# Two places of a weight ring exchanged, and the state part's preparation placed between the input blocks of a second mixer

## The chip, the cores and the metric

One core of a Trainium2 chip runs the whole program. The metric is the time of one execution on the device in microseconds (us), as the median of three runs.

## What is computed

The reference is two transformer-like blocks in a row, for 256 tokens of width 1024, in float32. Cut to what matters here:

```
x = first_block(x, ...)      # mixer (attention + rwkv7), then f = (silu(h@w_ffn_gate) * (h@w_ffn_up)) @ w_ffn_down
mod = silu(c) @ w_ada + b_ada               # six vectors of 1024: shifts, scales, gates
h = rms_norm(x) * (1 + sc1) + sh1
u, z, xbc, dt_raw = split(h @ w_in, ...)    # 256, 768, 1792 and 12 columns
y_pool = (pooled mean of u - u) @ w_pool * pool_scale
xbc = silu(causal_conv4(xbc) + bias)        # x: 768 channels, B: 512, C: 512
dt = softplus(dt_raw + dt_bias);  a_cs = cumsum(dt * -exp(a_log)) in chunks of 128 tokens
decay[l, s] = exp(a_cs[l] - a_cs[s]), l >= s          # per head, 12 heads
y = ((C B^T) * decay) @ (x * dt)  +  C @ state * exp(a_cs)   + x * d_skip
y = rms_norm_per_group(y * silu(z)) * norm_w
x = x + g1 * (concat(y_pool, y) @ w_out)
x = x + g2 * hier_moe(modulate(x))          # 32 experts, top 2 of one group of 8
out = rms_norm(x) * final_norm_w
```

## The kernel before

Everything runs from one hand-written program per engine; semaphores order them. There are 8 banks of matmul output memory. `plan_banks` lists all uses of the banks in the order in which TensorE writes them; use n is bank n mod 8, and TensorE may write it only when the use 8 places earlier has been read out.

**The ring of weights.** The list `W` names all weight blocks (up to 2 MB each) in the order of use, and SyncE (SP) loads block n into place `n % RING` of three. Before it issues a load, it waits until the last use of the block that lay in that place. SP works in order: a load that waits holds up all loads behind it. Around the feed-forward part the list is ... `("wo", 1)`, `("ff", 0)`, `("ada", 4)`, `("ff", 1)`, `("ff", 2)`, `("ff", 3)`, ... A block `("ff", c)` holds 256 gate and 256 up columns; `("ada", 4)` is a block of the modulation weights, used by TensorE in `ada_chunk(4)` just before the feed-forward part, while `("ff", 0)` is used by its first two of 22 steps.

**High and low parts.** Most products are made in three passes from rounded parts of both operands (lines 792 to 794). For each such block ScalarE (ACT) writes the rounded high part (`high_parts`, line 1684, two halves), and VectorE (DVE) writes the low part in place of the block in the ring (`low_part`, line 569, two halves). TensorE waits for the low part in `halved`.

**The second mixer.** Its input weights are six blocks `("in2", c)`, c = 0 to 5; 0 and 1 give `u` and `z`, two further blocks of 256 channels (`("xb", j)`, j = 0 to 6) lie in each of c = 2, 3, 4, and c = 5 (1072 KB) holds `("xb", 6)` and the 12 dt columns. TensorE makes `xb` 0 to 6; for each, ACT copies the bank into `xraw` and writes a scaled copy into `xs` (lines 1942 and 1945), DVE adds the three other taps of the convolution in six instructions (line 2583), and ACT applies silu (line 1952, the last at 1954). Then the dt product `("dt2",)` is made token by token with 12 columns a matmul, followed by the pooling `("pl",)` (lines 1336, 1338), `ada_chunk(6)` (line 969), the cumulative sums `("cs",)` (lines 1345, 1346), the pooled map `("pm",)` (1351), the decay rows `("rb", i, q)` (line 1359; DVE reads them at 2609, ACT takes the exponential at 1973), the products C B^T `("cb", i)` (line 1367; DVE masks them at 2616 and multiplies the decay by them at 2620), transposes of x and B (line 1373; ACT copies at 1978, DVE scales by dt at 2624), and the first product of the scan, `y_diag(0)` (line 1388). The latter needs the decay times C B^T and the scaled x. Two halves of the token rows (i = 0, 1) follow, then the output product `("mx", i, n)`, the norm and the router.

**The experts.** After the mixer SP streams the weights of 32 experts through two sets of buffers, one in the ring and one in the arena. The first set is loaded after the mixer's last norm sums and after `mx`; each later load waits for TensorE's use of the one before (`next_w13`, line 674; `next_w2`, line 680).

## Time and profile before

| what | value |
|---|---|
| median of 3 runs | 1127.08 us (1125.91 to 1128.21) |
| the profiled execution | 1125.6 us |
| its span, first to last instruction | 1123.8 us |
| TensorE (PE) busy | 1048.3 us, 93% of the span |
| DVE, ACT, GpSimd (POOL) busy | 462.5, 353.3, 39.6 us |
| HBM read | 314.37 MB |
| mean granted TensorE clock | 0.99 of full |
| chain that ended last | PE 70%, DMA 21%, DVE 4%, ACT 2% |

The table is from the profile's page. Times in the rows further down count from the first instruction of the span. "Busy" is the time in which an engine had an instruction at work; the idle time in square brackets behind a row is how long the engine stood before it, and "<-" names what released it. A clock of 1.00 is TensorE's upper level, 2.4 GHz, and 0.50 its lower one, 1.2 GHz.

### The profile page before, as it was taken

The page shows a single profiled execution, that of the slowest core. Times are in us where ns is not written, and L with a number is a line of the kernel's source. Part 1 is how long each engine was busy: PE and PEld are TensorE (multiplying, and loading weights), DVE is VectorE, ACT ScalarE, POOL GpSimd, SP SyncE. Part 2 cuts the span into 40 slices and gives each one's busy share as a digit, 9 for nine tenths or more (in the row PEclk, how much of TensorE's full clock was granted, in tenths as well). Part 3 has the DMA queues.
Part 4 walks back from the last instruction along what each step waited for, and adds up shares of the span by engine and source line. Part 5 has one row for each costly group of instructions (what it writes and reads, how often), then busy time and mean ns, then how long its engine had stood idle before and what let it go on. Part 6 is the DMA issues. An engine that isn't in the chain of part 4 may idle for free.

```text
span 1123.8 us, 17871 instructions
## 1 busy us (share of the span) xinstructions
PE 1048.3 (93%) x7527; PEld 717.3 (64%) x7527; DVE 462.5 (41%) x699; ACT 353.3 (31%) x507; POOL 39.6 (4%) x32
## 2 busy tenths in 40 slices
PE   6999999999989999999999999999899989898986
PEld 5996779899789998867986453443244333242432
DVE  4784245567634544356757351222122212121212
ACT  5752323554444444265542220111011111010102
POOL 0002200002000100000000000000000000000000
PEclk9999999999989999999989999999999999999999
DMA  9454371147474636675366869999999999999994
GB/s 324 157 203 159 110 247 60 71 155 265 148 225 152 216 122 228 232 288 181 119 222 244 363 255 422 420 423 421 422 423 421 422 422 423 421 422 422 422 421 191
DMA packets 95301, 316.36 MB, mean 282 GB/s; under 512 B 8118, under 2 KB 33030, under 8 KB 70534
## 3 DMA queue, kind: packets, MB, share of 16 engines
q1 hardware_dynamic: 94198, 312.75, 72.2%
q10 hardware_dynamic: 1040, 2.69, 0.7%
q8 instruction: 50, 0.82, 0.3%
q14 instruction: 13, 0.11, 0.0%
HBM read 314.37 MB, written 1.05 MB: 281 GB/s over the span
## 4 chain that ended last, share of the span: by engine, by line
PE 70%; DMA 21%; DVE 4%; ACT 2%; issue 1%; SPq 0%; POOL 0%; DVEq 0%; ACTq 0%
DMA arena<-in_w 20%; PE bank L1513 12%; PE bank L792 11%; PE bank L794 11%; PE bank L793 11%; PE bank L1537 4%; PE bank L778 4%; PE bank L1053 3%; PE bank L969 1%; PE bank L1493 1%; PE bank L1002 1%; PE bank L769 1%; PE bank L1550 1%; PE bank L739 1%; DVE ring_low L569 1%
## 5 line engine op out<-in xcount | busy, mean ns | idle before, releaser
L1513 PE MATMUL bank<-ring,hT 128*64 128x512 f32 x512 | 226.6, 594 | 28.7 <-DMA arena<-in_w 27.6
L1513 PE MATMUL bank<-arena,hT 128*64 128x512 f32 x512 | 226.7, 594 | 0.0
L794 PE MATMUL bank<-h_high,ring_low 128*128 128x256 f32 x688 | 194.1, 282 | 0.0
L1513 PEld LDWEIGHTS bank<-ring,hT 128*64 128x64 f32 x512 | 67.9, 137 | 180.4 <-issue 130.6
L569 DVE TENSOR_TENSOR ring_low<-ring,hi_high 128x2048 fp32r<-128x2048 f32 (+2 forms) x58 | 126.3, 2220 | 106.2 <-ACT hi_high L1684 106.2
L792 PE MATMUL bank<-h_high,hi_high 128*128 128x256 f32 x528 | 150.1, 284 | 4.9 <-DVE ring_low L569 4.2
L793 PE MATMUL bank<-h_low,hi_high 128*128 128x256 f32 x528 | 148.7, 282 | 0.0
L1684 ACT ACTIVATE hi_high<-ring 128x2048 fp32r<-128x2048 f32 (+2 forms) x58 | 104.6, 1853 | 101.8 <-DMA ring<-in_w_ffn_up 45.1
L794 PEld LDWEIGHTS bank<-h_high,ring_low 128*128 128x128 f32 x688 | 131.2, 191 | 0.0
L1537 PE MATMUL bank<-arena 128*64 128x512 f32 x384 | 113.3, 595 | 7.1 <-DVE hT L2821 6.7
L2827 DVE TENSOR_TENSOR arena<-arena,bank 128x512 f32<-128x512 f32 x16 | 17.3, 1083 | 229.3 <-ACT arena L2045 229.3
L792 PEld LDWEIGHTS bank<-h_high,hi_high 128*128 128x128 f32 x528 | 100.5, 190 | 6.3 <-DVE ring_low L569 4.4
L793 PEld LDWEIGHTS bank<-h_low,hi_high 128*128 128x128 f32 x528 | 100.8, 191 | 0.3 <-issue 0.2
L2045 ACT ACTIVATE arena<-bank 128x512 f32<-128x512 f32 x16 | 9.6, 599 | 231.1 <-PE bank L1513 231.1
L1513 PEld LDWEIGHTS bank<-arena,hT 128*64 128x64 f32 x512 | 67.9, 137 | 0.0
L1537 PEld LDWEIGHTS bank<-arena 128*64 128x64 f32 x384 | 35.1, 137 | 40.5 <-issue 39.5
L1537 PE MATMUL bank<-ring,arena 128*64 128x512 f32 x128 | 56.6, 595 | 4.3 <-ACT arena L2049 4.3
L2841 DVE SCALAR_TENSOR_TENSOR con<-bank,small,arena 128x512 f32<-128x512 f32 x32 | 24.0, 751 | 86.3 <-PE bank L1537 86.3
L2054 ACT ACTIVATE y_high<-con 128x512 fp32r<-128x512 f32 x32 | 20.2, 631 | 125.1 <-DVE con L2841 125.1
L792 PE MATMUL bank<-h_high,hrw_high 128*128 128x256 f32 x160 | 45.8, 286 | 0.5 <-DVE ring_low L569 0.5
L793 PE MATMUL bank<-h_low,hrw_high 128*128 128x256 f32 x160 | 45.3, 283 | 0.0
L1537 PEld LDWEIGHTS bank<-ring,arena 128*64 128x64 f32 x128 | 16.9, 137 | 37.6 <-issue 36.1
(404 smaller groups left out, 1694.2 us busy)
## 6 DMA issues: line engine op xcount, KB each, us to landing
arena<-in_w SPq DMA_DIRECT2D x112, 1024.0 KB, 22.7
ring<-in_w SPq DMA_DIRECT2D x80, 1024.0 KB, 20.3
ring<-in_w_in SPq DMA_DIRECT2D x12, 2048.0 KB, 8.3
ring<-in_w_ada SPq DMA_DIRECT2D x8, 2048.0 KB, 8.2
ring<-in_w_ffn_gate SPq DMA_DIRECT2D x11, 1024.0 KB, 5.5
ring<-in_w_ffn_up SPq DMA_DIRECT2D x11, 1024.0 KB, 8.7
ring<-in_w_ffn_down SPq DMA_DIRECT2D x5, 2048.0 KB, 7.9
ring<-in_w_in SPq DMA_DIRECT2D x12, 512.0 KB, 4.6
```

Source lines behind the costliest of these rows:

```text
L569: return eng.tensor_tensor(ring_lo[:, r, c0:c1], ring[:, r, c0:c1], high_of(n)[:, c0:c1].bitcast(F32), ALU.subtract)
L778: last = mm(ps[:, 0:512], lhs[k][:, i * P:(i + 1) * P], w[:, k, 0:512], start=(k == 0), stop=(k == nk - 1))
L792: mm(ps, a[0], b[0], start=start, stop=False)
L793: mm(ps, a[0], b[1], start=False, stop=False)
L794: return mm(ps, a[1], b[0], start=False, stop=stop)
L1053: last = mm(ps[r, j * w:(j + 1) * w], left(4 * q + j, r), right(4 * q + j, r), start=True, stop=True)
L1513: last = mm(both(6 + half, x), hg[:, k, (2 * q + x) * CAP:(2 * q + x + 1) * CAP], w13s[x][k // 4][:, k % 4, half * EF:(half + 1) * EF], st ...
L1537: last = mm(both(4 + n, x), acT[:, 0, f, x * CAP:(x + 1) * CAP], w2s[q][x][f // 2][:, f % 2, n * 512:(n + 1) * 512], start=(f == 0), stop= ...
L1684: A_(high_of(n)[:, f], ring[:, r, f], ACT.Copy).then_inc(S("high"), 1)
L2054: A_(y_hi[n], y_out[:, n, :], ACT.Copy).then_inc(S("y_high"), 1)
L2827: V.tensor_tensor(by_row(ac[:, 0, :]), in_rows(sa[:, 0, :]), in_rows(bank[7][:, :]), ALU.mult).then_inc(S("ac"), 1)
L2841: V.scalar_tensor_tensor(y_out[:, n, :], bank[4 + n][:, :], slot_gate[:, 0:1], g2[:, n * 512:(n + 1) * 512], ALU.mult, ALU.mult).then_inc( ...
```

## The change

1. From `("ff", 2)` on, ring places 1 and 2 are exchanged (`ring_slot`). `("ff", 2)` now lies where `("ada", 4)` was, and `("ff", 3)` where `("ff", 0)` was. All later blocks keep their distance of three.
2. The input blocks of the second mixer are loaded in the order 0, 1, 5, 4, 3, 2, and `xb` is made from 6 down to 0, so that C, B and the dt columns come first.
3. The dt product is made channel by channel (24 matmuls of 256 columns over the last 128 columns of the block, then a copy by ACT and two transposes) instead of 48 matmuls of 12 columns.
4. dt, the pooling, the cumulative sums, the decay rows and C B^T stand between the `xb` blocks on all three engines.
5. The low parts of the last two blocks, in2 3 and in2 2, are split: DVE makes the first half, GpSimd the second.
6. Buffers move in the arena (`dec`, `cbm`, `dif`, `acs`, `ysq` and others), since they now live at the same time as the weights' high parts; `ada_chunk(6)` comes behind `xb` 0, and `ada_sum(6)` before the last transposes.

```diff
+IN2 = (0, 1, 5, 4, 3, 2)
...
-        for c in range(6):
+        for c in IN2:
             stream(("in2", c), [(0, cols(w_in2, c * 512, min(c * 512 + 512, w_in2.shape[1])))],
-                   ("uz", 1, c) if c < 2 else ("xb", 2 * c - 3) if c < 5 else ("dt2",))
+                   ("uz", 1, c) if c < 2 else ("xb", 2 * c - 4))
...
+        keys = [key for key, _, _ in W]
+        turned, kept = (keys.index(key) % RING for key in (("ada", 4), ("ff", 0)))
+
+        def ring_slot(n):
+
+            return {turned: kept, kept: turned}.get(n % RING, n % RING) if n >= keys.index(("ff", 2)) else n % RING
...
             for n, (key, parts, last) in enumerate(W):
-                r = n % RING
+                r = ring_slot(n)
...
-                    pe.wait_ge(S("in2_low"), 2 * (n - BY_TWO) + 2)
+                    pos = n - BY_TWO
+                    pe.wait_ge(S("in2_low"), 2 * pos + 2 if pos < 4 else pos + 5)
+                    if pos >= 4:
+                        pe.wait_ge(S("in2_pool"), pos - 3)
```

TensorE's program from the end of `uz`, with the new functions' bodies as before except `dt_rows` (the removed lines are those that stood behind `xb`):

```diff
+            def dt_rows():
+
+                halved(("in2", 5))
+                w = parts_view(("in2", 5), "p (k c) -> p k c", k=KD)
+                ps = write(pe, ("dt2",))
+                for k in range(KD):
+                    last = by_parts(ps[:, 0:SEQ], [x[:, k, DT_AT:DT_AT + P] for x in w], (hT_hi[2][:, k, :], hT_lo[:, k, :]),
+                                    k == 0, k == KD - 1)
+                last.then_inc(*full(("dt2",)))
...
+            dt_rows()
+            xb(6)
+            drained(pe, ("dt2",))
+            transposes(("dtt",), [(i, dtrow[:, i * P:(i + 1) * P]) for i in range(NT)])
+            xb(5)
+            pooled()
+            xb(4)
+            decay_sums()
+            decay_rows(0)
+            xb(3)
+            decay_rows(1)
+            xb(2)
+            xb(1)
+            pe.wait_ge(S("xs"), 4)
             for i in range(NT):
...
+                gram(i)
+            xb(0)
+            ada_chunk(6)
+            pe.wait_ge(S("xs"), 5)
             for i in range(NT):
...
+                x_tokens(i, 1)
```

ACT's, DVE's and GpSimd's programs, cut to the order of the calls (`raw` is the copy and the scaled copy of a bank, `silu_of` the silu of the n-th block made, `conv` the six taps):

```diff
+            ps = filled(act, ("dt2",))
+            A_(dtrow, ps[:, 0:SEQ], ACT.Copy).then_inc(*free(("dt2",)))
+            high_parts(BY_TWO + 4)
+            raw(6)
...
+            raw(5)
+            high_parts(BY_TWO + 5)
+            silu_of(0)
+            raw(4)
+            silu_of(1)
+            raw(3)
+            silu_of(2)
...
+            decay_exp(0)
+            raw(2)
+            decay_exp(1)
+            silu_of(3)
+            raw(1)
+            silu_of(4)
+            silu_of(5)
+            raw(0)
+            ada_rows(6)
+            for i in range(NT):
+                tokens_out(i, 1)
+            silu_of(6)
...
+            for n in (BY_TWO + 4, BY_TWO + 5):
+                _, words = split_words(n)
+                pool.wait_ge(S("high"), 2 * n + 2)
+                low_part(nc.gpsimd, n, words // 2, words).then_inc(S("in2_pool"), 1)
...
+            first_half_low(BY_TWO + 4)
+            conv(6)
...
+            conv(5)
+            first_half_low(BY_TWO + 5)
...
+            decays(0)
+            conv(4)
+            conv(3)
+            decays(1)
+            conv(2)
+            conv(1)
```

The order on two engines, as the built programs have it (instructions in program order; the same line has a number some 13 to 45 higher on TensorE and some 10 to 95 higher on DVE in the changed kernel; `con` holds constants, `arena` the buffers, `bank` the matmul outputs).

TensorE, before, from `ada_chunk(6)` behind the pooling up to `y_diag(0)`:

```order
L969 MATMUL bank<-ring,arena 32x512 x8
L1345 MATMUL bank<-arena,con 128x12 x2
L1346 MATMUL bank<-arena,con 128x12
L1351 MATMUL bank<-arena 64x256 x4
L1359 MATMUL bank<-con,arena 128x128 x24
L1367 MATMUL bank<-arena 128x128 x8
L1373 MATMUL bank<-con,arena 128x128 x16
L939 MATMUL bank<-con,arena 64x1 x8
L969 MATMUL bank<-ring,arena 32x512 x8
L1388 MATMUL bank<-arena 128x64 x12
```

TensorE, changed, from the end of the last block `xb` 0 (L805 to L807) up to `y_diag(0)` (L1433):

```order
L806 MATMUL bank<-h_low,hi_high_49 128x256
L807 MATMUL bank<-h_high,ring_low 128x256
L982 MATMUL bank<-ring,arena 32x512 x8
L1351 MATMUL bank<-con,arena 128x128 x4
L1417 MATMUL bank<-arena 64x256 x4
L1351 MATMUL bank<-con,arena 128x128 x4
L952 MATMUL bank<-con,arena 64x1 x8
L1351 MATMUL bank<-con,arena 128x128 x8
L982 MATMUL bank<-ring,arena 32x512 x8
L1433 MATMUL bank<-arena 128x64 x12
```

The sums, decay rows and C B^T (L1345, L1359, L1367 before) no longer stand between the last block and `y_diag(0)`; the transposes, the modulation chunks and the pooled map do.

DVE, before, from the last block's convolution on:

```order
L2583 SCALAR_TENSOR_TENSOR arena<-arena,parcol 128x255 x2
L2583 SCALAR_TENSOR_TENSOR arena<-arena,parcol 128x254 x2
L2583 SCALAR_TENSOR_TENSOR arena<-arena,parcol 128x253 x2
L2591 TENSOR_TENSOR arena<-bank,small 128x2x12
L2594 SCALAR_TENSOR_TENSOR arena<-arena 128x2x12
L2596 COPY arena<-bank 128x512
L2598 SCALAR_TENSOR_TENSOR arena<-arena 128x2x12
L2600 SCALAR_TENSOR_TENSOR arena<-arena,small 128x2x12
L2602 COPY arena<-bank 128x3x12
L2609 TENSOR_SCALAR arena<-bank,arena 128x128 x24
L2616 TENSOR_TENSOR arena<-bank,con 128x512
L2620 TENSOR_TENSOR arena<-arena 128x1536
```

DVE, changed, from the dt step on (L2684 is the old L2591, L2664 the convolution's old L2583, L579 the low part's old L569):

```order
L2684 TENSOR_TENSOR arena<-bank,small 128x2x12
L2687 SCALAR_TENSOR_TENSOR arena<-arena 128x2x12
L579 TENSOR_TENSOR ring_low<-ring,hi_high_51 128x2048
L2664 SCALAR_TENSOR_TENSOR arena<-arena,parcol 128x255 x2
L2664 SCALAR_TENSOR_TENSOR arena<-arena,parcol 128x254 x2
L2664 SCALAR_TENSOR_TENSOR arena<-arena,parcol 128x253 x2
L2691 SCALAR_TENSOR_TENSOR arena<-arena 128x2x12
L2693 SCALAR_TENSOR_TENSOR arena<-arena,small 128x2x12
L2664 SCALAR_TENSOR_TENSOR arena<-arena,parcol 128x255 x2
L2664 SCALAR_TENSOR_TENSOR arena<-arena,parcol 128x254 x2
L2664 SCALAR_TENSOR_TENSOR arena<-arena,parcol 128x253 x2
L579 TENSOR_TENSOR ring_low<-ring,hi_high_49 128x2048
```

The dt steps, which stood behind all seven convolutions, now stand around the first, and each of the two low parts left is one half, with a convolution ahead of or behind it; the other halves are GpSimd's.

## Rows read from the trace of the kernel before

**Rows 1.** Windows (us; busy us and count of PE, PEld, DVE, ACT, POOL; PEclk; DMA share; GB/s).
```profile
326.00:333.00 7.00, 6.12 (x28) 6.12 (x29) 4.44 (x5) 4.84 (x6) 1.28 (x1) 0.51 0.75 238
...
569.00:579.00 10.00, 10.00 (x51) 6.33 (x51) 2.32 (x8) 3.74 (x6) 0.00 (x0) 0.51 0.49 168
...
666.00:1101.00 435.00, 396.48 (x1924) 164.42 (x1920) 91.13 (x146) 51.16 (x88) 0.00 (x0) 1.00 1.01 420
```
**Rows 2.** Timeline of SP's queue (start us, us, engine, line, what), 286 to 345 and 524 to 530.
```profile
288.50 0.37 SPq L654 DMA_DIRECT2D ring<-in_w_ffn_gate  x1
...
525.26 0.37 SPq L654 DMA_DIRECT2D ring<-in_w_in  x1
```
**Rows 3.** Chain of waits, 284 to 350 (start us, us, what).
```profile
311.23 0.37 SPq L654
311.64 8.72 DMA ring<-in_w_ffn_up
320.39 1.93 ACT hi_high L1684
322.33 4.50 DVE ring_low L569 x2
```
**Rows 4.** Waits of PE, 326 to 500 (us in total, times, longest).
```profile
PE bank L792 <- DVE ring_low L569: 4.2, 1, 4.2
```
**Rows 5.** Timeline of PE (idle before, releaser in brackets).
```profile
288.40 1.92 PE L969 MATMUL bank<-ring,arena 128*32 128x512 f32 x16
...
565.49 0.17 PE L792 MATMUL bank<-hi_high,h_high 128*128 128x12 f32 x1
...
572.91 1.13 PE L1336 MATMUL bank<-arena 128*64 128x256 f32 x4
...
575.73 3.39 PE L969 MATMUL bank<-ring,arena 128*32 128x512 f32 x16
...
580.83 5.62 PE L1359 MATMUL bank<-con,arena 128*128 128x128 f32 x48
...
588.07 1.91 PE L1373 MATMUL bank<-con,arena 128*128 128x128 f32 x16
...
...
593.58 2.86 PE L1388 MATMUL bank<-arena 128*128 128x64 f32 x24 [0.72 <-DVE arena L2616]
```
**Rows 6.** Timeline of DVE.
```profile
526.73 4.49 DVE L569 TENSOR_TENSOR ring_low<-ring,hi_high 128x2048 fp32r<-128x2048 f32 x2
...
561.58 2.71 DVE L2583 SCALAR_TENSOR_TENSOR arena<-arena,parcol 128x255 f32<-128x255 f32 x6 [2.95 <-ACT arena L1945]
567.23 2.70 DVE L2583 SCALAR_TENSOR_TENSOR arena<-arena,parcol 128x255 f32<-128x255 f32 x6 [2.94 <-ACT arena L1945]
...
582.09 6.29 DVE L2609 TENSOR_SCALAR arena<-bank,arena 128x128 f32<-128x128 f32 x24 [1.98 <-PE bank L1359]
...
589.09 1.76 DVE L2620 TENSOR_TENSOR arena<-arena 128x1536 f32<-128x1536 f32 x1
```
**Rows 7.** Timeline of ACT.
```profile
532.94 3.72 ACT L1684 ACTIVATE hi_high<-ring 128x2048 fp32r<-128x2048 f32 x2 [6.48 <-DMA ring<-in_w_in]
...
569.97 0.63 ACT L1954 ACTIVATE arena<-arena 128x512 f32<-128x512 f32 x1 [2.25 <-DVE arena L2583]
573.57 1.28 ACT L1958 ACT_TABLE_LOAD   x1 [2.97 <-DVE arena L2594]
...
585.40 1.48 ACT L1973 ACTIVATE arena<-arena 128x1536 f32<-128x1536 f32 x1 [2.81 <-DVE arena L2609]
```
**Rows 8.** GpSimd's instructions grouped by shape (count, busy us, mean ns of one).
```profile
L2130 POOL TENSOR_TENSOR f_low<-arena,f_high 128x512 fp32r<-128x512 f32 x11 | 14.1, 1286 | 154.9 <-ACT f_high L1878 154.9
```
**Rows 9.** Timeline of DVE and POOL where both were at work, 267 to 269.
```profile
267.39 1.29 DVE L2468 TENSOR_TENSOR merged_low<-arena,merged_high 128x256 fp32r<-128x256 f32 x2
268.88 0.43 DVE L2468 TENSOR_TENSOR merged_low<-arena,merged_high 128x256 fp32r<-128x256 f32 x1 [0.20 <-ACT merged_high L1857]
...
267.55 0.84 POOL L2125 TENSOR_TENSOR arena<-arena 128x256 f32<-128x256 f32 x1 [0.59 <-DVE arena L2475]
```

More of the change, by code:

```diff
@@ L221, in plan_banks @@
     for i in range(NT):
-        o += [("mt", i, a) for a in range(2)] + [("as", 8) if i == 0 else ("ad", 9), ("mx", i, 0)]
+        o += [("mt", i, a) for a in range(2)] + [("as", 8) if i == 0 else ("ad", 9)] + [("mx", i, 0)]
         o += [("as", 9)] if i else []
@@ L1311, in _, with xb @@
             ada_sum(11)
-            for j in range(7):
+            def xb(j):
                 c = 2 + j // 2
@@ L1341, in _ @@
-            ada_chunk(6)
-            pe.wait_ge(S("da"), 1)
-            ps = write(pe, ("cs",))
-            for i in range(NT):
-                mm(ps[:, i * 16:i * 16 + SH], K("causal"), da[:, i, :], start=True, stop=True)
-            mm(ps[:, 32:32 + SH], K("after"), da[:, 0, :], start=True, stop=True).then_inc(*full(("cs",)))
+            def dt_rows():
[6 more added lines that the diff above has]
+                last.then_inc(*full(("dt2",)))
@@ new lines, in gram, with x_tokens @@
+            def gram(i):
+                ps = write(pe, ("cb", i))
+                for g in range(GRP):
+                    t = slice(i * P, (i + 1) * P)
+                    last = mm(ps[:, g * P:(g + 1) * P], xs[:, 6 + g, t], xs[:, 10 + g, t], start=True, stop=True)
+                last.then_inc(*full(("cb", i)))
+            def x_tokens(i, a):
+                transposes(("xt", i, a), [(c, xs[:, 4 * a + c, i * P:(i + 1) * P]) for c in range(4 if a == 0 else 2)])
+            dt_rows()
+            xb(6)
```

187 lines of the change are left out of this document (94 added, 93 removed), and 6 rows, old and new, of the table PLACED.

## The prediction

> **What bounds the kernel.** I read the windows by stage first, then the chain of waits, then TensorE's timeline around the places of the change, and last DVE, ACT and GpSimd there. The last stage, the experts, is bound by its weights: from 666 to 1101 the DMA share is 1.01 at 420 GB/s, while PE is busy 396 of 435 us [rows 1]. The amount streamed is fixed and the stream starts when the experts' first products free their buffers, so what is won ahead of 666 moves the end by the same amount, and nothing in the experts' stage needs to be faster. Ahead of it TensorE is what counts. It stands or runs slow at two places. The first is in the feed-forward part: the chain passes through a DMA of 8.72 us, the high half (1.93) and the low parts (4.50) of block `("ff", 2)` [rows 3], and PE waits 4.2 us for it [rows 4]. The granted clock is 0.51 in the window behind that wait [rows 1]. The second is between the last input block of the second mixer, which ends at 565.49, and the first product of the scan at 593.58 [rows 5]: 28.1 us in which PE is busy but with small pieces, and from 569 to 579 at a clock of 0.51 [rows 1].
>
> **The places of the ring.** The load of `("ff", 2)` is issued at 311.23, when `("ff", 0)` has been used up [rows 3]. In the changed kernel it takes the place of `("ada", 4)`, whose product starts at 288.40 and takes 1.92 us [rows 5]. SP has issued `("ff", 1)` at 288.50 [rows 2] and has nothing else ahead, so the load goes out at about 290.4, 21 us earlier. With the same 8.7 us for the DMA, at most as much again for the one ahead of it, and 6.4 us for the parts, it is ready by 315; PE asks for it at 322.7 (326.9 less the 4.2 us). Late next is `("ff", 3)`, which now waits for `("ff", 0)`: issued at 311.2, landed at about 320.4, low parts at about 326.8, wanted one block (96 matmuls of 0.118 = 11.3 us; 0.118 is 5.65 us between two blocks' convolutions [rows 6] over 48 matmuls) after 322.7, at 334.0. It has 7 us to spare. So the wait goes, 4.2 us. With it goes the slow clock, if that came from the wait: between 326.9 and 333.0 PE ran 28 matmuls, which at full clock are 3.3 us instead of 6.1. That is 2.8 us more, **7.0 us** together. If the clock falls anyway, 4.2 us are left.
>
> **The second mixer, as TensorE's sum.** Before: 28.1 us from the last block to `y_diag(0)`. After: the same pieces are counted wherever they stand. The new dt product is 24 matmuls of 0.118 = 2.8 us, against 565.49 to 572.91 = 7.4 us for the old [rows 5]; its two transposes are 0.2 (1.91 us for 16 records [rows 5]); the pooling is 1.4, half of its 2.8 us at the slow clock (572.91 to 575.73); sums 0.6 (with the pooled map they fill 579.1 to 580.8); decay rows 5.6; C B^T 1.7 (up to 588.07) [rows 5]. These are 12.3 us, all ahead of or between the blocks. Behind the last block, `xb` 0, there is a chain: 1.7 us from the block's end to the start of its convolution (565.49 [rows 5] to 567.23), 2.7 us of convolution [rows 6], silu until 570.6 [rows 7], so 5.1 us; then eight transposes (1.0 us) and `ada_chunk(7)` (1.92 us, as the chunk at 288.40). That is 8.0, with a semaphore's passing 8.2 us, and ACT's copies and DVE's scaling of the tokens end at about the same time by the same rows. What PE has beside it (`ada_chunk(6)`, four transposes, the pooled map, B's transposes, `ada_sum(6)`) is about 5 us and fits under the 5.1. So 12.3 + 8.2 = 20.5 us instead of 28.1: **7.6 us** if nothing waits inside. DVE's decay multiplications (two of 1.76 us [rows 6]) lie ahead of the last convolution and under PE's last block.
>
> **Does something wait inside?** Taking 525.9 as the start (565.49 less seven blocks of 5.65), PE would be through with `xb` 6 at 534.4, 5 at 540.3, 4 at 547.3, 3 at 556.4, 2 at 564.8 and 1 at 570.5. The weights arrive in time: the load issued at 525.26 [rows 2] is now in2 3, its high parts run from 532.94 for 3.72 us [rows 7], and it is wanted at 550.7; in2 2 is issued at 534.4 and wanted at 564.8. In2 4 is ready when DVE's row of 526.73 ends, at 531.2 [rows 6], and wanted at 534.6; in2 5 is earlier still. The table loads of ACT (1.28 us each [rows 7]) grow from three to five, under cover of the blocks.
>
> What is new is GpSimd beside DVE. No row shows it on a half block of 2048 columns; 512 columns take it 1.286 us [rows 8], so 5.1 us by four. And where both worked at once, two of DVE's instructions on buffers took 1.29 us, where one alone takes 0.43; the second ended 0.29 us after GpSimd's, at 268.68 [rows 9]. I read this as DVE standing until GpSimd is done when both of its inputs are buffers, as they are in the convolution. It is the nearest row; its lower end is no cost at all, its upper one the whole of GpSimd's time, twice 5.1 us. I take the upper. Then DVE goes: first half of in2 3 until 537.1; convolution 6 held until 542.2, done 544.9; dt steps; convolution 5 and the first half of in2 2, with the second hold, until 555.4; two copies; decay rows (3.15 us, half of 6.29 [rows 6]) until 559.5; two convolutions until 564.9; decay rows until 568.0. ACT takes the exponential (1.48 [rows 7]), a table load (1.28) and the silu of B (0.63) until 571.5. PE wants B at 570.5, for C B^T. It waits about 1 us, and DVE arrives 0.2 us late at the last convolution: **1.2 us** lost. On its engine the last block and all behind it are queued behind that wait.
>
> The Trainium skill, page "SBUF — State Buffer", section "Who interferes with whom", says that a DVE instruction with two inputs in SBUF and a GpSimd instruction that reads SBUF exclude each other, and the second to come is blocked until the first has finished. By that rule the sum is the one with 1.2 us lost, 13.4; if a meeting cost only what the one row shows, about 0.4 us, it would be 14.6.
>
> **The sum.** 7.0 + 7.6 - 1.2 = 13.4 us. Against the profiled execution's 1125.6 us this gives 1112.2; the median of the three runs, 1127.1, stands 1.5 us above that, which gives 1113.7. I forecast **1113.5 us**. A measurement of this kernel can tell about 0.2%, 2.3 us, from no change.
>
> **Rivals.**
> - GpSimd doesn't hold DVE. For it: only one short meeting is in the trace, and its price was small. Then DVE is about 9 us ahead, nothing waits, and the time is 1127.1 - 14.6 = 1112.5. Chance 0.2.
> - Only one of the two parts pays. The state part's order on ACT is tight: exponential, table loads and silus stand in one row behind each block's copies, and one that is late holds PE at C B^T or `y_diag(0)`. If 7.6 us are lost that way, 7.0 are left: 1120.1. Or the exchanged place doesn't bring the load forward (a wait ahead of it in SP's queue that the rows don't show): 6.4 are left, 1120.7. Against both: the distances above. Chance 0.12.
> - The clock falls at another place. In the trace it fell behind an idle stretch and behind the 12-column matmuls [rows 1]; both go, but behind `xb` 0 PE has transposes and one-column products for some 8 us. Ten slow microseconds cost 5: 1118.7. Against: the same pieces ran from 579 to 594 without it. Chance 0.08.
> - Slower: GpSimd's halves are much longer than four times the 512-column row. DVE stands twice for a time P; it has 9.2 us to spare before C B^T is late (10.2 cost 1.0), so the loss is 2P - 9.2 us. It passes the 14.6 us gain at P = 11.9 us, 2.3 times my 5.1. At P = 15 the time is 1127.1 - 14.6 + 20.8 = 1133.3. For it: DVE may in turn hold GpSimd. Against: eleven instructions of the same kind all have the same 1.286 us. Chance 0.04.
>
> **The numbers.** The forecast has the remaining 0.56. Its own range comes from the clock's 2.8 us and the 1.2 us either way, and from the medians' spread of 1 us: 1109 to 1117.5. To hold 8 in 10, the range takes in the second rival's neighbour, the clock, up to 1119.5, and leaves the 1120 cases and the slow one outside: 1109 to 1119.5. Faster by over 0.2% (below 1124.8) hold all cases but the last: 0.94; 0.02 for a sum that just cancels; 0.04 slower.
>
> **What would show it.** Right: no wait of PE for `ring_low` near 322, no slow clock behind it; the load of `("ff", 2)` near 290; `y_diag(0)` some 14 us earlier than 593.6, 21 to 22 us behind the end of what was `uz` plus seven blocks; convolution 6 starting only when GpSimd's instruction ends, and GpSimd's two instructions near 5.1 us each; a wait of PE at C B^T of about 1 us for ACT's silu; 435 us from the first refill of the experts to the last, as before. Wrong: a wait at C B^T or at a block's low part of several us, a window below 1.00 of the clock between 560 and 600, or an experts' stage that takes longer than before.

## The result, and the profile of the changed kernel

| what | before | changed |
|---|---|---|
| median | 1127.21 us (4 runs, 1125.91 to 1128.21) | 1113.09 us (4 runs, 1111.25 to 1115.47) |
| ratio, 95% interval | | 0.988 [0.9862, 0.9898] |
| profiled execution, and its span | 1125.6, 1123.8 us | 1114.15, 1112.4 us |
| mean granted TensorE clock | 0.99 | 0.997 |

The forecast was 1113.5 us, with a range of 1109.0 to 1119.5. The time fell by 1.2%, inside the range. What follows asks whether it fell for the reasons given.

The page of the changed kernel, its first lines (busy us, share of the span, instructions) and the shares of the chain that ended last:
```profile
span 1112.4 us, 17834 instructions
## 1 busy us (share of the span) xinstructions
PE 1041.5 (94%) x7505; PEld 711.4 (64%) x7505; DVE 465.4 (42%) x697; ACT 356.7 (32%) x510; POOL 49.7 (4%) x34
...
PE 72%; DMA 21%; DVE 3%; ACT 2%; issue 1%; SPq 0%; POOL 0%; DVEq 0%; ACTq 0%
```
PE has fewer busy microseconds than before (1041.5 against 1048.3): time at the lower clock counts as busy time, and the new dt product is shorter. GpSimd has 10.1 us more (49.7 against 39.6): its two new instructions.

Windows of the changed kernel. Columns as in [rows 1]: busy us and count of each engine, clock, DMA share, GB/s.
```profile
326.00:333.00 7.00, 7.00 (x61) 7.00 (x60) 2.15 (x3) 0.98 (x2) 1.29 (x1) 1.00 0.89 292
560.00:569.00 9.00, 9.00 (x78) 9.00 (x78) 5.17 (x14) 6.84 (x10) 0.00 (x0) 1.00 0.68 234
569.00:581.50 12.50, 12.50 (x112) 8.43 (x110) 9.62 (x16) 6.52 (x13) 0.00 (x0) 1.00 0.55 190
596.00:600.00 4.00, 4.00 (x7) 1.60 (x6) 2.54 (x6) 0.21 (x1) 0.00 (x0) 0.57 1.08 413
654.00:1089.00 435.00, 396.13 (x1922) 164.33 (x1920) 91.05 (x146) 51.15 (x88) 0.00 (x0) 1.00 1.01 420
```
Both slow stretches of [rows 1] are gone: the clock is 1.00 from 326 to 333, and from 560 up to `y_diag(0)` at 581.50. A short one stands at 596. In the experts' stage a window of the same 435 us shows the same PE time and the same DMA share as before; how long the stage takes is in the table below.

Waits of PE, first in 284 to 350, then in 500 to 620 (us in total, times, longest):
```profile
PE bank L959 <- DVE arena L2564: 1.0, 1, 1.0
PE bank L805 <- DVE h_low L2270: 0.7, 1, 0.7
...
PE bank L805 <- issue: 0.7, 1, 0.7
PE bank L788 <- issue: 0.5, 1, 0.5
PE bank L952 <- ACT arena L1842: 0.4, 1, 0.4
```
"issue" stands for a wait whose releaser the profile doesn't show. The 4.2 us of [rows 4] for `ring_low` are not among them, nor is any wait for the silu of B.

SP's queue in the changed kernel (start, us, line, what), which gives the places of the loads:
```profile
290.00 0.37 SPq L664 DMA_DIRECT2D ring<-in_w_ffn_gate  x1
...
291.89 0.56 SPq L664 DMA_DIRECT2D ring<-in_w_ffn_gate  x1
...
324.24 0.37 SPq L664 DMA_DIRECT2D ring<-in_w_ffn_gate  x1
335.76 0.37 SPq L664 DMA_DIRECT2D ring<-in_w_ffn_gate  x1
...
404.88 50.67 SPq L664 DMA_DIRECT2D ring<-in_w_ffn_down  x6
466.06 0.37 SPq L664 DMA_DIRECT2D ring<-in_w_in  x1
```
`("ff", 2)` is issued at 291.89 instead of 311.23 [rows 3]. Each later load is issued when a block has been used up, so the rows are also a clock of PE's progress. With the same rows of before they give this account (times from the start of the span):

| stretch | before | changed | gained |
|---|---|---|---|
| up to the load of `("ff", 1)` | 288.50 | 290.00 | -1.5 |
| to the first load of `down` (feed-forward blocks) | 120.55 | 114.88 | 5.7 |
| to the first load of `in2` | 60.74 | 61.18 | -0.4 |
| to the load behind the last `uz` | 55.47 | 54.16 | 1.3 |
| to `y_diag(0)` | 68.32 | 61.28 | 7.0 |
| to the experts' first refill | 72.84 | 73.09 | -0.3 |
| to the end | 457.4 | 457.8 | -0.4 |
| sum | 1123.8 | 1112.4 | 11.4 |

The entries are of one profile each. The first stretch is the same program in both, so its 1.5 us is the difference of two executions; without it the two profiles differ by 12.9 us. Two entries were foreseen in kind, 5.7 for the ring (forecast 7.0) and 7.0 for the state part (forecast 6.4, that is 7.6 less 1.2); 1.3 us was not foreseen.

PE's timeline in the changed kernel around the small pieces that now lie between blocks, and behind the last block. The blocks' own rows are left out.
```profile
542.68 0.51 PE L1371 MATMUL bank<-arena,con 128*128 128x12 f32 x4
...
543.27 2.92 PE L1378 MATMUL bank<-con,arena 128*128 128x128 f32 x24
...
565.94 1.95 PE L1386 MATMUL bank<-arena 128*128 128x128 f32 x16
...
573.55 1.92 PE L982 MATMUL bank<-ring,arena 128*32 128x512 f32 x16
...
579.64 1.92 PE L982 MATMUL bank<-ring,arena 128*32 128x512 f32 x16
581.50 0.77 PE L1433 MATMUL bank<-arena 128*128 128x64 f32 x5
```
None has an idle time in brackets. The last block ends at 573.55 and `y_diag(0)` starts at 581.50: 7.95 us, forecast 8.2. C B^T starts at 565.94 without a wait.

DVE in the changed kernel, then (second fence) two of its single instructions, from shorter windows, and (third) GpSimd:
```profile
530.38 2.28 DVE L579 TENSOR_TENSOR ring_low<-ring,hi_high 128x2048 fp32r<-128x2048 f32 x1
533.13 6.46 DVE L2664 SCALAR_TENSOR_TENSOR arena<-arena,parcol 128x255 f32<-128x255 f32 x6 [0.47 <-ACT arena L1991]
...
539.82 6.97 DVE L2664 SCALAR_TENSOR_TENSOR arena<-arena,parcol 128x255 f32<-128x255 f32 x6
546.72 2.28 DVE L579 TENSOR_TENSOR ring_low<-ring,hi_high 128x2048 fp32r<-128x2048 f32 x1
```
```profile
533.13 4.25 DVE L2664 SCALAR_TENSOR_TENSOR arena<-arena,parcol 128x255 f32<-128x255 f32 x1 [0.47 <-ACT arena L1991]
...
542.04 4.75 DVE L2664 SCALAR_TENSOR_TENSOR arena<-arena,parcol 128x253 f32<-128x253 f32 x1
```
```profile
531.78 5.31 POOL L579 TENSOR_TENSOR ring_low<-ring,hi_high 128x2048 fp32r<-128x2048 f32 x1 [98.26 <-ACT hi_high L1728]
541.69 4.82 POOL L579 TENSOR_TENSOR ring_low<-ring,hi_high 128x2048 fp32r<-128x2048 f32 x1 [4.60 <-ACT hi_high L1728]
```
GpSimd takes 5.31 and 4.82 us for 2048 columns, where DVE takes 2.28. A convolution's six instructions take 2.70 us alone [rows 6]; beside GpSimd they take 6.46 and 6.97. The single rows show how: one instruction of each six is stretched from 0.48 to 4.25 and 4.75 us and ends 0.29 and 0.28 us behind GpSimd (537.38 against 537.09, 546.79 against 546.51). The other five run at their usual length. So DVE does stand, once per operation of GpSimd and until that is over.

GpSimd stands for DVE as well. Its first operation starts while DVE's own low half, which also has two buffers as inputs, is still at work. Five profiles (four of them of runs described below) have this meeting:

| profile | GpSimd starts | DVE's half ends | overlap | GpSimd takes | less the overlap |
|---|---|---|---|---|---|
| changed | 531.78 | 532.66 | 0.88 | 5.31 | 4.43 |
| `r_state` | 536.20 | 537.24 | 1.04 | 5.49 | 4.45 |
| `r_after` | 531.54 | 532.27 | 0.73 | 5.17 | 4.44 |
| `r_warm` | 531.41 | 532.14 | 0.73 | 5.16 | 4.43 |
| `r_pace` | 533.00 | 533.97 | 0.97 | 5.41 | 4.44 |

The remainder is the same in all five, and near half of the 9.02 us that 4096 columns take when DVE is idle at the start (`r_pool`, below).

### The profile page after: what moved, and what is told of

Read it like the earlier page. It is cut to its first block, busy times and chain, and to the rows that moved or that the text cites. A ratio compares the mean times of both kernels' runs of the same rounds, so it can differ in the third digit from the quotient of the medians.

```text
span 1112.4 us, 17834 instructions
## 1 busy us (share of the span) xinstructions
PE 1041.5 (94%) x7505; PEld 711.4 (64%) x7505; DVE 465.4 (42%) x697; ACT 356.7 (32%) x510; POOL 49.7 (4%) x34
## 4 chain that ended last, share of the span: by engine, by line
PE 72%; DMA 21%; DVE 3%; ACT 2%; issue 1%; SPq 0%; POOL 0%; DVEq 0%; ACTq 0%
DMA arena<-in_w 20%; PE bank L1557 12%; PE bank L805 11%; PE bank L806 11%; PE bank L807 11%; PE bank L1581 4%; PE bank L788 4%; PE bank L1066 3%; PE bank L982 2%; PE bank L1537 1%; PE bank L1015 1%; PE bank L779 1%; PE bank L1594 1%; PE bank L749 1%; PE bank L1378 0%
## 5 line engine op out<-in xcount | busy, mean ns | idle before, releaser
L807 PE MATMUL bank<-h_high,ring_low 128*128 128x256 f32 x696 | 195.9, 281 | 0.0
L579 DVE TENSOR_TENSOR ring_low<-ring,hi_high 128x2048 fp32r<-128x2048 f32 (+2 forms) x56 | 121.7, 2217 | 100.4 <-ACT hi_high L1728 100.4
L805 PE MATMUL bank<-h_high,hi_high 128*128 128x256 f32 x536 | 153.8, 287 | 0.7 <-DVE h_low L2270 0.7
L806 PE MATMUL bank<-h_low,hi_high 128*128 128x256 f32 x536 | 151.9, 283 | 0.0
L807 PEld LDWEIGHTS bank<-h_high,ring_low 128*128 128x128 f32 x696 | 132.5, 190 | 0.0
L805 PEld LDWEIGHTS bank<-h_high,hi_high 128*128 128x128 f32 x536 | 101.0, 188 | 2.1 <-issue 2.1
L805 PE MATMUL bank<-h_high,hrw_high 128*128 128x256 f32 x160 | 45.8, 286 | 0.4 <-DVE ring_low L579 0.4
```

The costliest lines, as they stand in the source:

```text
L579: return eng.tensor_tensor(ring_lo[:, r, c0:c1], ring[:, r, c0:c1], high_of(n)[:, c0:c1].bitcast(F32), ALU.subtract)
L805: mm(ps, a[0], b[0], start=start, stop=False)
L806: mm(ps, a[0], b[1], start=False, stop=False)
L807: return mm(ps, a[1], b[0], start=False, stop=stop)
```

## The experiments

All were timed beside the kernel before on the same chip, in four groups: r_ring, r_state, r_dve, r_pool (median of before 1125.99, 16 runs); r_after, r_dve_b, r_uz, r_da (1125.63, 13 runs); r_fill, r_warm, r_best (1125.52, 17 runs); r_pace (1126.07, 7 runs).

### 1. The two parts alone

`r_ring` is the kernel before with this and nothing else:
```diff
+        def ring_slot(n):
+
+            return {turned: kept, kept: turned}.get(n % RING, n % RING) if n >= keys.index(("ff", 2)) else n % RING
...
-                r = n % RING
+                r = ring_slot(n)
```


> The kernel before with the exchange of the two ring places alone. By the prediction's term it is 7.0 us faster (the wait of 4.2 us and 2.8 us of slow clock). My theory after reading the two traces: TensorE's 256-column passes keep one of two paces, 117.8 ns or 120.0 ns apart; the kernel before went over to 117.8 behind the slow clock at 333, and without the stall it stays at 120.0 through the feed-forward part, so 1.8 us of the 7.0 are given back: 5.2 us faster, with 120.0 ns in the trace. If the pace goes to 117.8 without the stall too, the theory falls and 7.0 is right.

Measured: 1119.88 us (1117.92 to 1122.1), ratio 0.9945 [0.9928, 0.9963], 6.1 us under before. In its profile the feed-forward stretch takes 114.88 us, as in the changed kernel, with the slower of the two paces throughout (its loads are 11.52 us apart; section 3 below).

`r_state` is the changed kernel without it:
```diff
-            return {turned: kept, kept: turned}.get(n % RING, n % RING) if n >= keys.index(("ff", 2)) else n % RING
+            return {turned: kept, kept: turned}.get(n % RING, n % RING) if n >= len(keys) else n % RING
```


> The changed kernel without the exchange of the ring places (state part's preparation, order of the input blocks and GpSimd's halves as changed). The prediction's terms: 7.6 less 1.2, so 6.4 us faster than before. My theory after reading the traces: there is no wait at C B^T, and a wait of 1.0 us in front of u and z's second product also goes, because the third block is the small one: 8 to 9 us faster. The two single changes should add up to the changed kernel's 14 us within the noise of about 1 us; if they add up to clearly more or less, they share something.

Measured: 1119.18 us (1115.79 to 1123.68), ratio 0.9937 [0.9916, 0.9959], 6.8 us under before. Its wait of PE in 300 to 345, and the window behind it:
```profile
PE bank L805 <- DVE ring_low L579: 3.8, 1, 3.8
```
```profile
328.00:332.00 4.00, 4.00 (x23) 4.00 (x22) 1.77 (x1) 4.00 (x4) 1.29 (x1) 0.57 0.98 308
```
The parts add: 6.1 and 6.8 are 12.9 us; the changed kernel, timed again as `r_after`, is 12.2 us under before, and the first timing gave 14.1. Each part pays by itself, and within that spread neither takes anything from the other. The 8 to 9 us expected of `r_state` show in its profile (54.18 and 61.27 us in the two stretches of the second mixer, 8.3 us less than before's), but not in the times, which give 6.8.

### 2. Is the ring's gain a wait and a slow clock, or one thing?

`r_fill` is the kernel before with PE kept at work in its wait. It moves nothing, and the wait for the data stays:
```diff
-                halved(("ff", c))
                 ps = write(pe, ("ff", f))
+                if f == 4:
+                    keep_busy(ps, 4)
+                halved(("ff", c))
```


> The kernel before with nothing moved: in its wait for the low half at the third feed-forward block PE multiplies the constants into the bank that it is about to write, four calls of about 0.86 us each, 3.4 of the 4.2 us. The wait itself stays, so only the clock term of the ring's 7.0 us can be won. Theory (wait 4.2 and slow clock 2.8 are separate, and the clock falls because PE stood still): the granted clock stays 1.0 through 326 to 333 and the time is 1.7 to 3.4 us under the kernel before. Rival: the clock falls there for another reason; then the slow stretch stays, and the time is the kernel's before within 0.5 us. Second point: the 256-column pace, which fell from 120.00 to 117.78 ns behind that slow stretch, should stay what it was from 302 on.

Measured: 1123.5 us (1120.16 to 1126.13, 12 runs), ratio 0.9987 [0.9971, 1.0003]. The two windows of `r_fill`, from the wait on:
```profile
322.40:326.60 4.20, 4.20 (x22) 2.76 (x21) 3.38 (x2) 4.17 (x5) 0.00 (x0) 1.00 1.09 346
326.60:333.00 6.40, 6.17 (x46) 5.34 (x45) 3.83 (x4) 4.89 (x7) 1.30 (x1) 1.00 0.94 297
```
The clock stays at 1.00 (46 matmuls in 6.4 us, where before had 28 in 7.0 [rows 1]), so the slow stretch did come from PE standing still. The time falls by 2.0 us, but the interval just reaches 1. In the profile the stretch from the load of `("ff", 1)` to the first of `down` is 118.8 us, against 120.55 before: 1.7 us gained. The slow clock had been priced at 2.8; section 3 of the experiments shows the missing part. As the intervals stand, that this gain reaches the end of the kernel isn't shown.

### 3. Where the ring's missing 1.3 us went: a second pace of the matmuls

The forecast was 7.0 us for the ring, the trace gave 5.7. The place is visible in the distance of two loads, which is that of 96 matmuls of 256 columns. In the changed kernel it is 335.76 - 324.24 = 11.52 us. Here are the loads of before behind its stall:
```profile
341.21 0.37 SPq L654 DMA_DIRECT2D ring<-in_w_ffn_gate  x1
352.52 0.37 SPq L654 DMA_DIRECT2D ring<-in_w_ffn_gate  x1
```
11.31 us. The granted clock is 1.00 in both. Taken from start to start, these matmuls are either 117.8 or 120.0 ns apart, never between, and for tens of microseconds in the same way. In before they are 120.0 apart up to the stall and 117.8 behind it; in the changed kernel they are 120.0 apart through the whole part. The forecast took 0.118 from before's blocks in the second mixer (561 to 567), and counted the rest of the feed-forward part as unchanged.

Is this a property of the program? It isn't. `r_da` (below) is the same program as the changed kernel up to 516, and its loads stand so:
```profile
312.01 0.37 SPq L664 DMA_DIRECT2D ring<-in_w_ffn_gate  x1
323.32 0.37 SPq L664 DMA_DIRECT2D ring<-in_w_ffn_gate  x1
...
402.46 50.22 SPq L664 DMA_DIRECT2D ring<-in_w_ffn_down  x6
```
11.31 us again, and 113.0 us from the load of `("ff", 1)` at 289.4 to the first of `down`. Against before's 120.55 that is 7.5 us gained, the forecast's 7.0 and a little. So the ring is worth 5.7 us at the slower pace and 7.5 at the faster one, and which of them a run has is not in the edit. Of the fourteen profiles of this study, `r_state`, `r_pool`, `r_da` and `r_pace` have the faster pace in the feed-forward blocks from 303 or 306 on, the other ten the slower. In `r_state` it turned from 117.8 to 120.0 across the stall, in before the other way; in `r_fill`, where the stall was filled, it did not turn there. A last run tried to turn it on purpose, with four other products near 310:
```diff
+                if f == 1:
+                    for _ in range(4):
+                        mm(ps[:, 0:512], w[0][:, 0, 0, 0:P], hT_hi[1][:, 0:2, :].rearrange("p k t -> p (k t)"), start=True, stop=True)
```


> The changed kernel with four 512-column products more ahead of the second feed-forward row of blocks (near 305), into the bank that is about to be written. They cost about 0.9 us. In six of the profiles of kernels with the exchanged ring the 256-column products run 120.00 ns apart from 302 on, in two 117.78 ns apart, with the same instructions up to there. Theory: the pace is drawn when the stream of products starts or is broken, so four other products may draw it anew; if the pace goes to 117.78 the next two blocks stand 11.31 us apart instead of 11.52 and the time is about 1 us under the changed kernel. Rival: the pace doesn't depend on what PE ran just before; then it stays 120.00 or was 117.78 already ahead of them, and the time is 0.9 us above.

Measured: 1112.32 us (1111.64 to 1113.25), ratio 0.9874 [0.9857, 0.989]. The matmuls were 117.8 ns apart already from 306, ahead of the products at 309, so this run says nothing on the question. What draws the pace is open.

### 4. Does GpSimd's help pay, and what does its length cost?

`r_dve` leaves GpSimd out and gives the two half parts back to DVE:
```diff
                 low_part(V, n, 0, words // 2).then_inc(S("in2_low"), 1)
+                dve.wait_ge(S("high"), 2 * n + 2)
+                low_part(V, n, words // 2, words).then_inc(S("in2_low"), 1)
...
-            for n in (BY_TWO + 4, BY_TWO + 5):
-                _, words = split_words(n)
-                pool.wait_ge(S("high"), 2 * n + 2)
-                low_part(nc.gpsimd, n, words // 2, words).then_inc(S("in2_pool"), 1)
```


> The changed kernel with both halves of the last two blocks' low parts on DVE, nothing on GpSimd. If GpSimd holds DVE for its whole time (theory), convolution 6 and 5 take 2.7 us each instead of 6.5 and 7.0, DVE has 2.3 us more work for each half but ends its decay rows some 3 us earlier, and since TensorE did not wait in the changed kernel, the time stays within 0.5 us. Rival (GpSimd's help is worth something): slower by 1 to 4 us, with a wait of TensorE for a low part or at C B^T.

Measured: 1111.72 us (1110.8 to 1113.58), ratio 0.9872 [0.9852, 0.9891]. DVE in `r_dve`:
```profile
530.35 4.49 DVE L579 TENSOR_TENSOR ring_low<-ring,hi_high 128x2048 fp32r<-128x2048 f32 x2
534.76 2.70 DVE L2660 SCALAR_TENSOR_TENSOR arena<-arena,parcol 128x255 f32<-128x255 f32 x6
...
540.30 4.49 DVE L579 TENSOR_TENSOR ring_low<-ring,hi_high 128x2048 fp32r<-128x2048 f32 x2
...
545.52 3.19 DVE L2672 TENSOR_SCALAR arena<-bank,arena 128x128 f32<-128x128 f32 x12
```
DVE reaches the decay rows at 545.52; in the changed kernel, with help, at 549.73. So the help makes DVE 4.2 us later. `y_diag(0)` starts at 581.47 here and at 581.50 there: neither lateness nor earliness is on the path.

`r_pool` goes the other way: the whole low part of both blocks to GpSimd.
```diff
-            first_half_low(BY_TWO + 4)
             conv(6)
...
             conv(5)
-            first_half_low(BY_TWO + 5)
...
-                low_part(nc.gpsimd, n, words // 2, words).then_inc(S("in2_pool"), 1)
+                low_part(nc.gpsimd, n, 0, words).then_inc(S("in2_pool"), 1)
```


> The changed kernel with the whole low part of the last two blocks on GpSimd, none on DVE. GpSimd's instruction doubles to about 9 us. If DVE stands for all of it (theory), convolution 6 ends about 4 us later and convolution 5 with its low half gone about 4.5 us later, ACT's silu of B comes 3.5 us after TensorE wants it, and the time is 3 to 4 us longer than the changed kernel's. If GpSimd costs DVE a fixed small price a meeting (rival), or nothing, DVE is ahead by 4.6 us, and the time stays the same.

Measured: 1125.37 us (1121.02 to 1126.85, 10 runs), ratio 1.0001 [0.9986, 1.0016]: all of the change's gain is gone. GpSimd, DVE, PE and PE's wait in `r_pool`:
```profile
528.22 9.02 POOL L579 TENSOR_TENSOR ring_low<-ring,hi_high 128x4096 fp32r<-128x4096 f32 x1 [97.69 <-ACT hi_high L1728]
538.08 9.03 POOL L579 TENSOR_TENSOR ring_low<-ring,hi_high 128x4096 fp32r<-128x4096 f32 x1 [0.85 <-ACT hi_high L1728]
```
```profile
529.57 18.73 DVE L2664 SCALAR_TENSOR_TENSOR arena<-arena,parcol 128x255 f32<-128x255 f32 x6 [2.62 <-ACT arena L1991]
...
548.43 0.18 DVE L2692 SCALAR_TENSOR_TENSOR arena<-arena,small 128x24 f32<-128x24 f32 x1
```
```profile
548.67 1.03 PE L1371 MATMUL bank<-arena,con 128*128 128x12 f32 x4 [9.34 <-DVE arena L2692]
```
Six instructions that take 2.70 us alone took 18.73. The first is held for 7.95 us, until 537.52; two run in the 0.84 us between GpSimd's operations, and the fourth is held for 9.04 us, until 547.39. Behind the convolution in DVE's order is `da`, and PE waits 9.3 us for it at the cumulative sums. Inside that wait the clock falls: it is at the lower level from 541.5 to 555.1, so 6.4 us of it lie behind the wait and cost 3.2 us. The recorded expectation, 3 to 4 us, had C B^T as the place that counts. In the trace the stretch from the load behind the last `uz` (516.71) to `y_diag(0)` (590.37) is 73.7 us, 12.4 more than the changed kernel's 61.28, and 9.3 and 3.2 account for it. The profiled execution, 1121.02 us, is the fastest of the ten: elsewhere it is 5.6 us shorter than the changed kernel's, with the faster pace of section 3 and no slow stretch near 596.

Is it the hold, or the place of `da` behind it? `r_da` is `r_pool` with two steps moved:
```diff
-            conv(6)
             dve.wait_ge(S("dt_ln"), 1)
...
             V.scalar_tensor_tensor(da, dtr, -1.0, cast(alog.unsqueeze(1), P, NT, SH), ALU.mult, ALU.mult).then_inc(S("da"), 1)
+            conv(6)
```


> The variant in which GpSimd takes the whole low part of the last two blocks, with DVE's two small steps for da ahead of the convolution of block 6 instead of behind it. Theory: what cost 12 us there was one queue position: the convolution stood still for GpSimd's two operations of 9.0 us one behind the other (18.7 us for six instructions), and da, behind it, released the cumulative sums 9.3 us late, and then the clock fell. With da ahead of it, it is held at most by the first GpSimd operation (until about 537), PE's cumulative sums come at about 541, so no wait there; the decays and the later convolutions are late instead by about 10 us, against some 16 us of room in before's order. So 1 to 5 us slower than the changed kernel, at most 1118. Rival: the hold itself costs the 12 us wherever da stands, since everything on DVE is 10 us late and PE waits at the decay rows' banks: 1123 to 1126.

Measured: 1117.27 us (1115.78 to 1118.72), ratio 0.9928 [0.9903, 0.9953]. DVE and PE's longest wait in `r_da`:
```profile
533.33 4.54 DVE L2689 SCALAR_TENSOR_TENSOR arena<-arena 128x24 f32<-128x24 f32 x1 [5.72 <-ACT arena L2015]
...
538.00 13.99 DVE L2664 SCALAR_TENSOR_TENSOR arena<-arena,parcol 128x255 f32<-128x255 f32 x12
```
```profile
PE bank L1378 <- DVE arena L2695: 2.7, 1, 2.7
```
An instruction of 24 columns takes 4.54 us, until GpSimd's first operation ends at 537.83; alone it takes 0.17. With `da` at 538 the cumulative sums are in time, and 8.1 of the 12 us come back. In the trace the same stretch is 67.0 us (517.37 to 584.41), 5.8 more than the changed kernel's: a wait of 2.7 us at the decay rows and a slow clock from 552.0 to 558.8, of which 6.2 us lie behind the wait and cost 3.1. The medians leave only 3.8 us; the faster pace of section 3, which its profile has in the feed-forward part (1.9 us less there), would cover the difference. So two steps of 0.17 us, at another place in DVE's queue, were worth 8.1 us by the medians and 6.6 by the stretch.

### 5. The unforeseen 1.3 us

Before, PE waits 1.0 us near 513 for a bank that ACT drains behind a high part of 3.77 us; in the changed kernel the third block of the second mixer is the small one, its high part takes 2.13 us, and the wait is gone. `r_uz` is `r_ring` with ACT's high part of that block put behind the drain:
```diff
             ada_rows(11)
-            high_parts(BY_TWO + 2)
...
                         A_(sz[:, i, 0:256], ps[:, POOL:512], ACT.Silu).then_inc(*free(("uz", i, 0)))
+                        if i == 0:
+                            high_parts(BY_TWO + 2)
```


> The kernel before with the ring exchange and one more thing: ACT's high part of the third input block of the second mixer is issued behind the drain of the first gate bank, as a smaller block would let it be. Theory of the extra 1.3 us of the state part: PE's 1.0 us wait at the gate rows for a bank that ACT drains late (after a high part of 3.77 us) is what the changed kernel lost by taking the small block third; so that wait is gone here too and the time is 1.0 to 1.3 us under the 1119.9 us of the ring exchange alone. Rival: the wait only moves, since the high part is then late for PE (it ends about 0.6 us later), and the time stays at 1119.9.

Measured: 1119.51 us (1117.05 to 1122.15), ratio 0.9945 [0.9924, 0.9966]: not to be told from `r_ring`. In the trace the wait is gone, and the stretch from the first load of `in2` to the one behind the last `uz` is 54.2 us, against 55.5 in `r_ring` and 54.16 in the changed kernel. Behind it `r_uz` loses 1.6 us again up to `y_diag(0)` (68.3 against 66.6), with a slow clock of 10.2 us from 564.0 where `r_ring` has 6.8. So the cause of the 1.3 us is shown at its place. That it reaches the end of the kernel isn't: the medians agree, and a slow stretch that is longer in one execution than in another would cover it.

### 6. The last slow stretch, and is there a better version?

The changed kernel has a slow clock from 596.1 to 599.5 in both of its profiles, `r_dve` in neither of its two. The first timings put `r_dve` 1.4 us under the changed kernel, so four runs asked whether that difference is real and whether it is this stretch. First both again:

> The changed kernel as it is, timed again beside its variants. Both theories: ratio to the kernel before between 0.986 and 0.990, some 13.4 us faster. It is here as the zero for the next three, and to see whether its profile shows the slower of the two matmul paces (120.00 ns for 256 columns) in the feed-forward blocks again: if the pace belongs to the program, it does; if it is chance, it may show 117.78 ns.

> The changed kernel with the second halves of the last two low parts on DVE, GpSimd idle there, timed again in more rounds. Theory: nothing on the path rests on GpSimd's 4.8 to 5.3 us, PE waits for neither version, so the two are equal within 0.5 us. Rival: the first run's 1.4 us in its favour is real, because DVE no longer stands still for about 8 us and its work frees banks earlier; then its ratio lies 0.001 below that of the changed kernel.

Measured: `r_after` 1113.46 us (1110.67 to 1114.41), ratio 0.9889 [0.987, 0.9909]; `r_dve_b` 1111.11 us (1108.99 to 1114.88), ratio 0.9873 [0.9852, 0.9895]. The second profile of the version without GpSimd has a slow stretch of 3.4 us at 631.5 instead.

Then both with a filler (a product of constants, which the kernel has for such places) where PE waits near 595:
```diff
+                if i == 0:
+                    keep_busy(write(pe, ("mx", 0, 0)), 1)
                 for a in range(2):
                     drained(pe, ("mt", i, a))
```


> The changed kernel with one more multiplication of constants (0.86 us) where PE waits near 595 for the transposed rows before the output projection. Both of its profiles so far show a slow clock there (596 to 599.5), which costs 1.7 us. Theory: that stretch hangs on PE's short and broken work just before it; the filler keeps the clock, costs at most 0.4 us (it is longer than the 0.5 us wait), and the time falls by about 1.3 us against the changed kernel. Rival: the stretch comes all the same or lands later, and the time is the changed kernel's plus 0 to 0.4 us.

> Both edits that could still help: low parts wholly on DVE, and the filler near 595. Its two profiles without the filler show no slow clock at 596, and it measured 1111.1 and 1111.7 us. Theory: what the version without GpSimd had over the changed kernel (1.4 to 2.3 us) was that stretch of the clock and nothing else; so here the filler brings nothing and costs up to 0.4 us, and this run, the one before it and 1111.4 us agree within 1 us. Rival: the two gains add, and the time is under 1110.5 us.

Measured: `r_warm` 1111.17 us (1108.94 to 1113.76), ratio 0.9876 [0.9853, 0.9899]; `r_best` 1112.91 us (1109.29 to 1114.45), ratio 0.989 [0.9866, 0.9913]. The window of `r_warm`:
```profile
596.00:600.00 4.00, 4.00 (x11) 1.72 (x10) 2.03 (x6) 0.21 (x1) 0.00 (x0) 1.00 1.07 414
```
The stretch is gone in `r_warm`'s profile, and from `y_diag(0)` to its end it takes 1.9 us less than the changed kernel's (1110.0 - 580.98 = 529.0 against 1112.4 - 581.50 = 530.9). But the two edits together measure no better than neither, 1.7 us above `r_warm` where at most 1 was expected. The four versions (the changed kernel, `r_dve`, `r_warm`, `r_best`) lie between 1111.1 and 1113.5 us with intervals that overlap. No version is shown to beat the changed kernel; `r_dve` is as fast with less code.

## Why the prediction was right, point by point

- **What bounds the kernel.** Right. From the experts' first refill to the end it took 457.8 us against 457.4, so what was won ahead of 666 came out at the end less 0.4 us.
- **The ring, 7.0 us.** The wait of 4.2 us is gone; the load went out 19.3 us earlier (21 forecast); the clock's fall hung on the wait, as `r_fill` shows. The size was 5.7 us in the trace and 6.1 in the times. What the sum left out is the pace: it took every block behind the stall to run as before's did, at 0.118 us per matmul, and the changed kernel's profile has 0.120 throughout. Where the pace is the faster one (`r_da`), the stretch gives 7.5.
- **The second mixer, 7.6 us.** By PE's timeline the small pieces are 12.1 us (12.3 forecast: dt product 2.9, its transposes 0.1, pooling 1.5, sums 0.6, decay rows 5.3, C B^T 1.7) and the tail 7.95 (8.2). That is 20.05 us against 28.1, a gain of 8.05. The seven blocks took 1.0 us longer than before's (40.97 against 39.97), some 0.6 of it the slower pace from 537 on. Net 7.0 us. Of the 8.05, some 5.0 are the lower clock of before's 568.5 to 578.7 (2.2 in the dt product, 1.3 in the pooling, 1.5 in `ada_chunk(6)`), 2.3 the new form of the dt product (5.2 us at the upper level against 2.9), and 0.7 the wait at `y_diag(0)`. Moving the other pieces between the blocks saved PE next to nothing of their own time (decay rows 5.3 us against 5.5, C B^T 1.7 against 1.8). The clock falls 2.1 to 4.5 us after the start of the 12-column products in all four profiles that have them behind the blocks (before, `r_ring`, `r_uz`, `r_fill`), with PE busy, for 6.8 to 10.2 us; in the ten others it falls nowhere between the blocks and `y_diag(0)` unless PE has waited. But no run has the new dt product at the old place, or the old one at the new place, so whether the form or the place kept the clock up is open.
- **The wait inside, 1.2 us.** This is the step that failed, by a small amount. The silu of B was done at 565.2, where the forecast's own frame, moved by the 5.4 us that the blocks start earlier, has 566.1; PE came at 565.94 instead of 565.1. Each side was off by 0.9 us and the wait is not there. Its mechanism is there, and its size was too large: the two convolutions took 6.46 and 6.97 us, 8.0 in excess of their 2.70, where the forecast had DVE stand for all of GpSimd's time, 10.2, since each operation of GpSimd had begun before the instruction that it held. The 5.1 us forecast for GpSimd itself came close by luck (5.31 and 4.82): 4.4 is its own part of the first, and 0.9 the wait for DVE's half, which the forecast did not have in its sum. The 1.2 us that was not lost there and the 1.0 us lost in the blocks cancel, which is why the sum for this part, 6.4, came within 0.6 of 7.0; that is luck. `r_state` has 6.8.
- **The rule on the shared port.** The sum that followed the Trainium skill's page "SBUF — State Buffer", section "Who interferes with whom" (the second to come is blocked until the first is done), was the right one as to DVE, and the trace agrees in the other direction too, by the table above. In the trace convolution 6 goes on when GpSimd ends at 537.09, and in `r_pool` six instructions took 18.73 us. It made no difference to the time of this kernel, as `r_dve` shows.
- **Rivals.** That GpSimd doesn't hold DVE fell: it does. That only one part pays fell: `r_ring` 6.1, `r_state` 6.8. The clock falling at another place came true in small: 596.1 to 599.5, 1.7 us. It is one of the prediction's own signs of being wrong, a window below 1.00 between 560 and 600; before has a like stretch at 643.6 to 647.0, so it cost nothing net. The slower rival was wrong in its break-even. It reckoned 2P - 9.2, with C B^T as the place where lateness counts, so at P = 9.05 a loss of 8.9 us, less what DVE saves by giving up its own halves. `r_pool` lost 12 us at that P. What it had missed is the step that stands right behind the held one (`da`), so that its place is the cumulative sums and not C B^T, and the slow clock behind the wait.
- **The number.** 1113.5 against 1113.09 is closer than the working was. The ring came out 1.3 us short in the trace and a gain of 1.3 us that nobody had forecast made up for it; the wait inside and the slower blocks cancelled; and the changed kernel's own runs span 4.8 us.

## What to carry to other kernels

A second engine's help has to be priced in the first one's queue: here two helpers of 5 us made DVE 4.2 us later, and with two of 9 us, what decided between a loss of 4 and one of 12 us was whether a two-instruction step that PE waited for stood ahead of the held instruction or behind it. A stall of the matmul engine had two prices here, its own length and the slow clock behind it, and filling it with idle products could win only the second. And a gain of a microsecond or two is read stretch by stretch, from one load's issue to another's, since the times of one and the same kernel lay up to 7 us apart in these runs.

## What was not expected of the hardware

- **Two paces of one matmul at one granted clock.** 256 columns in fp32r, 117.8 or 120.0 ns from start to start, with the same instructions and a granted clock of 1.00: 11.31 or 11.52 us for 96. It costs some 1.8 us over the feed-forward blocks. It changed across a stall in two profiles; what sets it wasn't found.
- **The hold is whole, width doesn't matter, and it goes both ways.** Every low-part operation of GpSimd looked at here held just one instruction of DVE, the next one with two buffers, until 0.28 us after its own end (0.04 in `r_da`'s first): 4.25, 4.75, 7.95, 9.04 and 9.16 us for instructions of 0.48, and 4.54 us for one of 24 columns that takes 0.17. `r_pool`'s gap of 0.84 us between two operations let two instructions through. In turn, GpSimd's first half took 5.16 to 5.49 us, and 4.43 to 4.45 of it behind the end of the DVE instruction that it met.
- **Slow stretches come and go.** They lasted 3.4, 6.8, 10.2 or 13.7 us, and the same instructions have them in one profile and not in the next: at 596 in the changed kernel and not in `r_dve`, at 198.8 in `r_uz` and at 158.7 in `r_pace` alone, in parts of the program that no edit touched. 3.4 us at half the clock is 1.7 us of work, if PE has work for all of it.
